# Attention layer: the reciprocal denominators of fourteen of seventeen blocks go through memory and come back as rows, and GpSimd scales the gated output two blocks at a time

## The reference, cut to what matters

```python
m = jnp.maximum(jnp.max(s, axis=-1), sk)
p = jnp.exp(s - m[..., None])
den = jnp.sum(p, axis=-1) + jnp.exp(sk - m)
o = jnp.einsum('bhgqk,bkhd->bqhgd', p, v.astype(jnp.float32))
return (o / jnp.transpose(den, (0, 3, 1, 2))[..., None]).astype(q.dtype)
...
return (o * jax.nn.silu(g)) @ w_out
```

## Time and profile before

| | |
|---|---|
| runs, median of 3 | 2758.2 us (2755.74 to 2758.96) |
| the profiled execution's own time | 2757.1 us |
| its span in the trace | 2755.4 us |
| granted clock over the span | 0.986 |
| PE / PEld busy | 97% / 85% |
| DVE / ACT / POOL busy | 46% / 31% / 24% |
| DMA | 213 MB, 26304 of 183978 packets under 512 B |

### The profile page before, as it was taken

How to read it: one execution, slowest core, us unless ns; L and a number is a source line. 1 busy time by engine, 2 the same in 40 slices (tenths; PEclk the granted TensorE clock), 3 DMA queues, 4 the chain that set the end, 5 groups by cost and what they waited for, 6 DMA issues and landing times.

```text
span 2755.4 us, 47969 instructions
## 1 busy us (share of the span) xinstructions
PE 2664.2 (97%) x17507; PEld 2334.5 (85%) x17507; DVE 1260.2 (46%) x3354; ACT 853.2 (31%) x2196; POOL 671.3 (24%) x928
## 2 busy tenths in 40 slices
PE   6899999999999997999999999999999999998998
PEld 3788888888888885887799999999999999998787
DVE  3656647465664747455224142423333342515533
ACT  3434526243452623222213131222213131313111
POOL 1522131122213113333004030212213040303432
PEclk8999999999999998999999999999999999999999
DMA  9512030211203022343013031212222030317343
GB/s 345 207 48 63 2 90 2 63 50 41 64 2 89 7 73 96 117 136 125 27 20 99 23 83 42 68 49 55 69 37 80 23 102 16 83 42 205 105 140 107
DMA packets 183978, 213.09 MB, mean 77 GB/s; under 512 B 26304, under 2 KB 131728, under 8 KB 181856
## 3 DMA queue, kind: packets, MB, share of 16 engines
q1 hardware_dynamic: 173792, 182.92, 23.5%
q10 hardware_dynamic: 9984, 27.37, 2.6%
HBM read 172.18 MB, written 38.07 MB: 76 GB/s over the span
## 4 chain that ended last, share of the span: by engine, by line
PE 57%; DVE 2%; issue 1%; DMA 1%; POOL 0%; SPq 0%; ACT 0%; DVEq 0%; POOLq 0%
PE psum L521 11%; PE psum L523 11%; PE psum L522 11%; PE psum L1357 2%; PE psum L1359 2%; PE psum L1358 2%; PE psum L2218 2%; PE psum L2283 2%; PE psum L1776 2%; PE psum L1778 2%; PE psum L1777 2%; PE psum L2286 2%; PE psum L2266 1%; PE psum L2209 1%; PE psum L2173 1%
## 5 line engine op out<-in xcount | busy, mean ns | idle before, releaser
L521 PE MATMUL psum<-h_hi,m_w_lo 128*128 128x384 f32 (+1 forms) x1600 | 594.9, 372 | 4.7 <-DVE m_w_lo L506 3.6
L523 PE MATMUL psum<-h_hi,m_w_hi 128*128 128x384 f32 (+1 forms) x1600 | 574.4, 359 | 0.0
L522 PE MATMUL psum<-h_lo,m_w_hi 128*128 128x384 f32 (+1 forms) x1600 | 573.8, 359 | 0.0
L521 PEld LDWEIGHTS psum<-h_hi,m_w_lo 128*128 128x128 f32 x1600 | 301.9, 189 | 29.6 <-issue 5.2
L523 PEld LDWEIGHTS psum<-h_hi,m_w_hi 128*128 128x128 f32 x1600 | 301.0, 188 | 27.0
L522 PEld LDWEIGHTS psum<-h_lo,m_w_hi 128*128 128x128 f32 x1600 | 302.3, 189 | 22.5
L521 PE MATMUL psum<-h_hi,attn_w_lo 128*128 128x384 f32 (+1 forms) x800 | 291.2, 364 | 0.4 <-DVE attn_w_lo L366 0.2
L523 PE MATMUL psum<-h_hi,attn_w_hi 128*128 128x384 f32 (+1 forms) x800 | 286.0, 358 | 0.0
L522 PE MATMUL psum<-h_lo,attn_w_hi 128*128 128x384 f32 (+1 forms) x800 | 285.6, 357 | 0.0
L831 ACT ACTIVATE arena<-arena,stats 128x640 f32<-128x640 f32 (+2 forms) x272 | 216.2, 795 | 150.2 <-DVE stats L902 150.2
L902 DVE CUSTOM_DVE_ANT_0 arena<-psum,wmask,nsk 128x640 f32<-128x640 f32 (+2 forms) x256 | 206.1, 840 | 53.9 <-PE psum L1073 47.0
(11 more groups left out here) (284 smaller groups left out, 4750.7 us busy)
## 6 DMA issues: line engine op xcount, KB each, us to landing
m_bc<-gate_rows_mlstm SPq DMA_DIRECT2D x128, 256.0 KB, 3.7
m_w_raw<-in_mlstm_w_in SPq DMA_DIRECT2D x40, 512.0 KB, 4.8
h_full<-gated_output SPq DMA_DIRECT2D x31, 512.0 KB, 4.1
gated_output<-gT SPq DMA_DIRECT2D x8, 1088.0 KB, 5.2
layer_output<-xb_out ACTq DMA_DIRECT2D x17, 512.0 KB, 2.7
h_hi_full<-layer_output SPq DMA_DIRECT2D x17, 512.0 KB, 4.7
out<-h_hi_full ACTq DMA_DIRECT2D x17, 512.0 KB, 4.9
xb<-in_x_sample ACTq DMA_DIRECT2D x16, 512.0 KB, 6.7
```

The costliest lines, as they stand in the source:

```text
L521: pe.matmul(out, self.lo[:, k, :], E.h_hi[:, k, tok], start=(k == 0), stop=False)
L522: pe.matmul(out, self.hi[:, k, :], E.h_lo[:, k, tok], start=False, stop=False)
L523: ins = pe.matmul(out, self.hi[:, k, :], E.h_hi[:, k, tok], start=False, stop=(k == KT - 1))
```

## The change

For blocks 0 to 13 of each sub-stage (seven pairs; `LONE` is 14) the spreading copy of GpSimd, the transpose of `rspr` on PE and one of the two operations of `gate` are gone. DVE writes the reciprocals of all 17 blocks into one `rden` (128 x 2 x 17). SP takes them in pairs of blocks through memory, in the new `recip_rows`: two stores, one for each head, of 128 x 2 values to `E.recip_dram`, where they lie by token; a wait until both have landed; then two loads which read a head's 256 values as a row into each of its 64 partitions (`spread_rows`, in `shuf`, two buffers). GpSimd multiplies two blocks of `gT` (128 x 256) by these rows, in the new `scale`. Blocks 14, 15 and 16 go as before, with one `rspr` buffer.

```diff
+                def recip_rows(kv, sub):
+                    i = kv * 2 + sub
+                    sp.wait_ge(s_rope, at(kv * ROPES + NG * (2 + sub)))
+                    with nc.allow_non_contiguous_dma(reason="reciprocals by row"):
+                        for r in range(PAIRS):
+                            cols = slice(2 * r * P, 2 * (r + 1) * P)
+                            sp.wait_ge(s_rd, at(i * NT + 2 * r + 2))
+                            for hh in range(2):
+                                sp.dma_start(E.recip_dram[i, hh, cols].rearrange("(b t) -> t b", t=P), rden[:, hh, 2 * r:2 * r + 2]).then_inc(s_rw, 16)
+                            sp.wait_ge(s_rw, at(32 * (i * PAIRS + r + 1)))
+                            if r >= 2:
+                                sp.wait_ge(s_scaled, at(i * PAIRS + r - 1))
+                            for hh in range(2):
+                                sp.dma_start(spread_rows[r % 2][HD * hh:HD * hh + HD, :], E.recip_dram[i, hh:hh + 1, cols].partition_broadcast(HD)).then_inc(s_rb[r % 2], 16)
...
                 def store(kv, sub):
+                    sp.wait_ge(s_scaled, at((kv * 2 + sub + 1) * PAIRS))
                     sp.wait_ge(s_og, at(kv * (2 * NT) + (sub + 1) * NT))
...
                     load_weights(kv, 3)
+                    recip_rows(kv, 0)
                     rotary(kv, 3, 0)
...
                         sp.dma_start(spare[:, 0:3, :], w_out[:, 0:3, :]).then_inc(s_wo, 16)
+                        recip_rows(kv, 1)
                         sp.wait_ge(s_S, at(NKV * (2 * NU)))
...
                         J.sp_load(sp, kv * 5 + 5, kv_columns(kv + 1))
+                        recip_rows(kv, 1)
                         rotary(kv + 1, 0, 0)
...
+                            def scale(r):
+                                i = kv * 2 + sub
+                                per = (PAIRS + 1 - r % 2) // 2
+                                g = gT[:, 2 * r * P:2 * (r + 1) * P]
+                                pool.wait_ge(s_rb[r % 2], at(32 * (i * per + r // 2 + 1)))
+                                pool.wait_ge(s_og, at(bbase + 2 * r + 2))
+                                settle(E, pool)
+                                pool.tensor_tensor(g, g, spread_rows[r % 2], ALU.mult).then_inc(s_scaled, 1)
...
                             for b in range(NT):
                                 if 2 <= b + 1 < NT:
                                     sink_less_max(b + 1)
-                                pool.wait_ge(s_rd, at(bbase + b + 1))
-                                pool.wait_ge(s_pv, at(bbase + (b - 1 if b >= 2 else 0)))
-                                settle(E, pool)
-                                pool.tensor_copy(rspr[:, b % 2, :, :], rden[:, b % 2, :].unsqueeze(2).to_broadcast([P, 2, HD])).then_inc(s_rs, 1)
+                                if b >= 5 and b % 2 == 1:
+                                    scale((b - 5) // 2)
+                                if b >= LONE:
+                                    pool.wait_ge(s_rd, at(bbase + b + 1))
+                                    pool.wait_ge(s_pv, at(bbase + b))
+                                    settle(E, pool)
+                                    pool.tensor_copy(rspr[:, :, :], rden[:, :, b].unsqueeze(2).to_broadcast([P, 2, HD])).then_inc(s_rs, 1)
                                 if b == 4 and m == 4 and not last:
                                     J.pool_hi(pool, kv * 5 + 5, kv * 6 + 8)
+                            scale(PAIRS - 1)
...
                     dve.wait_ge(s_rope, at(kv * ROPES + rope))
+                    if g == 0 and m != 1:
+                        dve.wait_ge(s_scaled, at((kv * 2 + (1 if m == 3 else 0)) * PAIRS))
...
                         def gate(b):
                             g = gT[:, b * P:(b + 1) * P]
                             dve.wait_ge(s_pv, at(bbase + b + 1))
+                            if b < LONE:
+                                dve.scalar_tensor_tensor(g, weighted, 0.5, g, ALU.mult, ALU.mult).then_inc(s_og, 1)
+                                return
...
                     def pv(b):
 
-                        pe.wait_ge(s_rs, at(bbase + b + 1))
                         pe.wait_ge(s_og, at(bbase + b))
-                        pe.transpose(spread, rspr[:, b % 2, :, :].rearrange("p h d -> p (h d)"), E.ident[:, :])
+                        if b >= LONE:
+                            pe.wait_ge(s_rs, at((kv * 2 + sub) * (NT - LONE) + b - LONE + 1))
+                            pe.transpose(spread, rspr[:, :, :].rearrange("p h d -> p (h d)"), E.ident[:, :])
```

More of the change, by code:

```diff
@@ L561, in phase_attn @@
         nsk = sb("nsk", [P, 4])
-        stats = sb("stats", [P, 6, 2, 2])
-        negm, rsum, sarg, esink, den, rden = (stats[:, x, :, :] for x in range(6))
-        rspr = sb("rspr", [P, 2, 2, HD])
+        stats = sb("stats", [P, 5, 2, 2])
+        negm, rsum, sarg, esink, den = (stats[:, x, :, :] for x in range(5))
+        rden = sb("rden", [P, 2, NT])
+        rspr = sb("rspr", [P, 2, HD])
         kvout = probT[0][:, 0, 0, :].rearrange("p (a d) -> p a d", a=2)
@@ L580, in phase_attn @@
         w_in = E.a["attn_w_in"][0].rearrange("(k p) m -> p k m", p=P)
+        spread_rows = [shuf[:, j * 2 * P:(j + 1) * 2 * P] for j in range(2)]
+        s_rw, s_scaled = sem("recip_stored"), sem("o_scaled")
+        s_rb = [sem(f"recip_rows_loaded{j}") for j in range(2)]
         NU = 2 * NT
+        PAIRS = 7
+        LONE = 2 * PAIRS
         kinds = ["kv", "q", "g", "q", "g"]
@@ L921, in denominators @@
                             dve.wait_ge(s_den, at(bbase + b + 1))
-                            dve.wait_ge(s_rs, at(bbase + (b - 1 if b >= 2 else 0)))
-                            dve.reciprocal(rden[:, p, :], den[:, p, :]).then_inc(s_rd, 1)
+                            if b == 0:
+                                dve.wait_ge(s_rw, at(32 * (kv * 2 + sub) * PAIRS))
+                                dve.wait_ge(s_rs, at((kv * 2 + sub) * (NT - LONE)))
+                            dve.reciprocal(rden[:, :, b], den[:, p, :]).then_inc(s_rd, 1)
                         def gate(b):
@@ L927, in gate @@
                             dve.wait_ge(s_pv, at(bbase + b + 1))
+                            if b < LONE:
+                                dve.scalar_tensor_tensor(g, weighted, 0.5, g, ALU.mult, ALU.mult).then_inc(s_og, 1)
+                                return
                             dve.scalar_tensor_tensor(g, spread, 0.5, g, ALU.mult, ALU.mult).then_inc(s_gr, 1)
-                            dve.wait_ge(s_gr, at(bbase + b + 1))
+                            dve.wait_ge(s_gr, at((kv * 2 + sub) * (NT - LONE) + b - LONE + 1))
                             dve.tensor_tensor(g, weighted, g, ALU.mult).then_inc(s_og, 1)
@@ L2315, in build @@
     E.ckt_dram = dram("cached_keys_turned", [P, NKV * PAST])
+    E.recip_dram = dram("reciprocals_by_token", [2 * NKV, 2, T])
     E.ogT_dram = dram("gated_output", [KT, P, T])
```

## The result

The changed kernel takes 3406.8 us (median of 4 runs, 3402.0 to 3419.0), the kernel before 2758.6 us beside it (4 runs): a ratio of 1.2359, 95% interval 1.2325 to 1.2393. It is slower, as forecast, but by 648 us and not by 150, and it lies above the range of 2790 to 3350.

The account below looks back on a forecast made before the run. PE, busy 97% of the span, was taken as the bound. Against 2757.1 us: -12.9 transposes, +139 stops, +5.9 last store, +2.4 weights, +16 clock, so +150.4 and 2907.5 us; range 2790 to 3350.

Parts of the forecast that it names:

- the cover: Attention sub-stage: 49.4 us from the first reciprocals until GpSimd reaches pair 5 (the sixth), during which its round trip is hidden.
- the give of 2.3 us: Attention blocks: slack of about 2.3 us, from ACT's `sink_exp` start and idle time, before late rows stop the sub-stage.
- The point from which it hurts: Attention sub-stages: landing time of a pair's stores above which late rows stop the sub-stage, put at 7.3 us.
- L: Time from SP's issue of a pair's two stores to the landing of both; taken as 10.2 us, ends 2.1 and 19.2.
- 6 L - 43.8: Stop of each attention sub-stage in us, if positive: 17.4 us at L = 10.2, +139 us in eight.
- 6 L + 7.9: Time in us from the first reciprocals at which pair 5's loaded rows are ready, in each attention sub-stage.
- The step that failed: Reciprocal stores to memory: two 512-byte stretches written as fast as one, so L = 10.2 and +139 us.
- the rival by number of values: Reciprocal stores: each value costs 35 ns, L = 19.2, 571 us of stops, 3333 us in total; chance 0.26.
- What is moved: 0: Rotary tables, `store` and later weights behind 28 SP DMAs, and `shuf` use: no cost before the last sub-stage.
- the tail: End of the last attention sub-stage: the store waits for pair 6's scaling until 81.0 instead of 75.1, +5.9 us.
- The weights' +2.4 us: Last attention sub-stage: output weights in SP's queue end 2.4 us after the reciprocals, delaying them by +2.4 us.
- the clock: PE in attention: idle time lowers the granted clock, 2 us a sub-stage, +16 us.

Follow-up runs that it names:

- the fifth experiment: Changed kernel storing only the first two pairs per sub-stage, with no row loads and GpSimd multiplying the gated output by itself: 2856.3 us, ratio 1.0364.

## Why the prediction was wrong, step by step

**The mechanism was right.** The stop of a sub-stage was put as what the sixth pair's rows are late beyond the cover and the give of 2.3 us. With what was measured it gives 120.0 - 47.5 - 2.3 = 70.2 us, 562 in eight. The cover was right too: 49.4 us against 47.5. The point from which it hurts, L = 7.3, is bracketed: pairs with 2.1 to 4.6 us cost nothing, the ones with 7.6 and 7.9 us do. But those cost 71 and 98 us where 6 L - 43.8 gives 14 and 29 in eight, so the true point lies lower. Late single pairs are not the reason, for the means of L are the same 7.6 and 7.9. The cycle is L + 1.4 and L + 1.5 there, so that the sixth product starts 56.5 and 60.5 us after the first reciprocals, 9 and 13 us late, where 6 L + 7.9 has 53.3 and 55.3; and 9 x 8 = 72 us is all of the first loss, with hardly any give (0.7 us in the mean).

**The step that failed** is "a store whose values alternate between two such stretches of 512 bytes takes as long as one with one stretch, and L = 10.2". Measured: 18.2 us in the median, 19.1 for the first pair, which is the rival by number of values, 19.2. The stretches are not written side by side; one store alone takes half. The reason given for the choice, that the place is what costs, was true all the same (2.1 us for the same values 64 bytes apart), but it did not carry the size: if the place costs, the number of values in it may still be what it costs by. Line 1900 wrote one store at a time into one stretch and could not tell the two apart; of the two sizes, the 35 ns worked out from its two stores was nearly right (18.2 / 512 = 36 ns), and that the second store did not run beside the first, which stood under the rival, was the better evidence.

**Mis-sized beside it.** The cycle was put at L + 1.0 and is L + 1.2 by the means (19.2 against 18.0), nearly right. The rows were put at 2.9 us behind their load's issue; the first pair's product starts 5.1 us behind it (209.14 to 214.2), since the second load is issued half a microsecond after the first and lands after more than 4 us, not 2.4. For the sixth pair, which counts, it is 5.6 us in the mean: 2.7 us a sub-stage, 22 us in all. Whether the stores behind the loads slow them, or the place that they read, no run separates.

**"What is moved: 0"** was wrong by 84 us. That sentence let pair 6 be scaled "about where a delayed sub-stage ends" and gave the projections as cover. At 19.2 us a cycle the seventh product starts 139 us after the first reciprocals, against 55.5 without a trip, the three projections are over and the rotary shuffle waits, as PE does behind it. Dropping the seventh pair took that wait away. In the last sub-stage the tail was put at 5.9 us and is 15.5 (30.1 against 14.6 at the output projection); the rival by number had 15 for it. The weights' +2.4 us can't be seen apart.

**The account**: the kernel without the trip, 2745.1, and 562 + 84 + 15.5 make 3406.6; measured are 3406.8. So close a fit is partly luck, for the terms are read to a microsecond a sub-stage only. But a count that takes no give from the forecast bears it out. From one sub-stage's first reciprocals to the next one's, the seven stretches are 573 us longer than in the kernel without the trip, 509 of them ahead of the sixth product and 64 behind it. With six pairs they are 395 us longer, 414 ahead of that product, so that 19 are won back behind it: a give of 2.7 us each. The wait for the seventh product so comes to 64 + 19 = 83 us. The stops of the fifth experiment have no term of their own; in the change they seem to lie inside the time in which the rows are late anyway. Nothing is left for **the clock** either, put at +16. It did fall as forecast (it was 1.00 at 150 to 1075 us before):

```profile
150.00:1740.00 1590.00, 1047.16 (x7662) 887.85 (x7661) 542.66 (x1435) 409.47 (x1077) 210.89 (x344) 0.80 0.20 33
```

(the columns are PE, PEld, DVE, ACT and POOL busy, then the granted clock). PE is busy for 140 us more than without the trip (2787.3 against 2647.4 us, as many instructions), 46 of them in the attention's projections. But while the rows set the pace, a PE that works for 1047 of 1590 us has time to be slower; how much of the 46 us lies beside the wait for the seventh product was not measured, so part of the 83 us may be the clock's.

**Right**: the 112 transposes at 0.115 us (12.2 measured, 12.9 put), the product of GpSimd as hidden work (0.73 us), no gain from DVE's and GpSimd's removed operations. The fixed cost that was weighed, about 2 us by the Trainium skill's "DMA: Bandwidth & Descriptors", section "Anatomy of one DMA", stays where the trace had put it: right for stores into places of their own, a ninth of the 18.2 us measured here.

## What to carry to other kernels

A DMA's bytes and pieces don't give its time: 512 values of 4 bytes take 18 us into packed memory, 2 us into places 64 bytes apart, and 2.7 us, in pieces of 8 bytes, into a row of SBUF. A transposition of small values by DMA should go through SBUF, which worked here as a whole; or it should leave gaps, though no run here reads spread values back, so that the price of this is not shown. When a nearby row shows a surprising price, look for two of the same kind in a row and take the price by number until a row says that they overlap. And when a chain sets the pace, ask what else stands behind its last link; here that was a buffer lent from the next stage.

## What the hardware showed that I had not expected

Slow writes are not only slow for those who wait for them. Four stores in each sub-stage whose data nobody used cost 111 us, through stops of DVE and ScalarE of up to 10.3 us that end on no engine, and of PE of up to 7.0 us, nearly all of which end when a pair's stores land. The stops came only where these took 16 us and more: in the runs with 2.1 to 7.9 us from stores to loads there is not one of DVE and ScalarE, and at 9.4 us, with one packed store a pair, just one, of 2.2 us. The packets of the instruction loads took up to 4.1 us instead of 1.65, but 3.8 us also where nothing stopped.

The packets themselves don't show the slowness. The 4-byte packets of the first pair's stores are recorded at 9 ns each at most and are over within a microsecond of their start; then SyncE's queue is silent until the landing, 17 us on. And the price is one of memory: the same packing of 8-byte pieces into a row of SBUF lands in 2.0 us.
